# The mixer's 31-tap convolution, all four channel tiles on TensorE with dense weights in groups of 32 channels

## The chip, the cores and the metric

The kernel runs on one core of one Trainium2 chip. The metric is the device time of one execution, in microseconds; smaller is better.

## The reference

Two transformer blocks follow each other on one sequence of 512 tokens, model width 1024, all in float32. The change is inside the second block's mixer. There the normed input is projected to queries, keys and values of a differential attention (4 heads, two softmaxes per head whose difference weighs the values, a rotary embedding on 16 of 64 dimensions) and to `u`, 1024 columns for a convolution branch:

```python
    c = u[..., :CV_WIDTH] * jax.nn.sigmoid(u[..., CV_WIDTH:])      # CV_WIDTH = 512
    c = causal_dwconv(c, cv_dw_w) + cv_dw_b.astype(c.dtype)         # 31 taps, one filter per channel
    c = jax.nn.silu(layernorm(c, cv_ln_g, cv_ln_b))
    y = jnp.concatenate([a, c], axis=-1)                            # a: the attention's output
    return jnp.einsum("bsc,cd->bsd", y, w_out)
```

## The kernel before

Activations lie transposed, channels on the 128 partitions and the 512 tokens along the free axis, so the 512 convolution channels are four tiles. Every float32 matrix product is three TensorE matmuls: each operand is split into a high part (the value cast to fp32r) and a low part (the rest), and high x high, high x low and low x high are added in PSUM. A 128x512 step of a projection is three matmuls of 512 columns; a weight unit of 128x1024 feeds 24 of them.

Weights come as such units, in the order of `unit_order` (L192). A ring of four slots holds them: SP loads `raw` (L2809, 512 KB), ScalarE casts it to `wh` (`hi`, L1379), GpSimd subtracts to get `wl` (`low`, L2710), and each of them may start on unit j + 4 once TensorE has used unit j (`refill`). SP works off one list in unit order; what else it has to move is put in front of a certain `raw(j)`, and that `raw(j)` waits until `wl` of unit j - 4 is there. So a DMA in front of `raw(p + 9)` is issued after `wl` of unit p + 4.

No planner decides anything: each engine has its program written out by hand, and the order of the calls is the order of its queue. The calls of one name in the five programs (`dproj`, `qk_d`, `turn_d`, `pv_d`) are one step's share on each engine.

The stretch in question goes as follows.

- **u and dv** (TensorE L907 to L918). Four times two projections `u(j)`, `u(4+j)` go to PSUM banks (0,1), (2,3), (4,5), (0,1). VectorE multiplies each by the norm's factor (L2363), ScalarE takes the sigmoid, VectorE multiplies the two. After tile 1 VectorE also scales X (`scale_x`, eight operations). `dv` makes the values in banks 2 to 5; `v_low` on VectorE makes their low parts.
- **The convolution.** Tiles 0 and 1 are done by VectorE: `taps(m)` (L2349) does m multiply-adds of 512 elements, 62 in all, spread over the steps. Tiles 2 and 3 are done by TensorE with diagonal weights: 31 taps x 3 matmuls of 512 columns for each, on shifted views of a padded tile, in sixteen halves (`cw`, L936) called as `conv(x)` between other work, two of them ahead of step 0's `qk_d(2)`, eleven in steps 0 to 8, the last in step 10.
- **Query and key projections** `dproj(h, step)` (L920, L2387): steps 0 and 1 are the halves of dq, 3 and 4 those of dk, all in bank 0. After step 1 ScalarE copies the bank to `rx` and issues four small DMAs that exchange rows for the rotary embedding (L1677); VectorE multiplies by the cosines (to TM5), then in step 2 by the sines, adds, casts, subtracts. After step 4 ScalarE copies to `rth`, VectorE makes `rtl`, and TensorE's step 5, the rotation ("rot"), multiplies by a permutation; the same four VectorE operations follow.
- **The attention loop** of 16 steps n (head n // 4, row block n % 4; L1073, L1735, L2486). In step n TensorE does `qk_d(n + 2)`, half a projection while n < 10, and `turn_d(n)`, the transpose of the weights; in even steps also `pv_d(n // 2 - 1)`. ScalarE does the exponentials of n + 2, copies the transpose (`ath`) and scales for n + 1; VectorE the maxima of n + 2, the low part of the transpose (`atl`) and the difference of the two softmaxes of n + 1. `pv_d` needs `atl` of both of its steps. From step 10 on, keys and values of the memory fill TensorE's time.
- After step 9 the layer norm adds the four convolved tiles `AC`.

Of the kernel before, what the change touches and what calls it, by code (L numbers as in the profile page):

```python
# [7 lines left out]
F32 = mybir.dt.float32  # L8
# [7 lines left out]
P = 128  # L16
# [152 lines left out]
CW_HALVES = (2, 2, 1, 1, 1, 1, 1, 1, 1, 0, 1, 0, 0, 0, 0, 0)  # L169

KV_STEP = 10
CW_BEFORE = 4
TAP_STEPS = (3, 3, 3, 3, 3, 3, 2, 2, 0, 0, 0, 0, 0, 0, 0, 0)
assert CW_BEFORE + sum(CW_HALVES) == 16

# [16 lines left out]
def unit_order():  # L192
# [18 lines left out]
    done = CW_BEFORE  # L211
    for n in range(16):
        step = D_STEP.get(n, (0, 0))
        more = [("cw", 2 + x // 8, x // 2 % 4) for x in range(done, done + CW_HALVES[n]) if x % 2]
        done += CW_HALVES[n]
        u += [(("dq", "dk")[step[1] // 3], step[0])] if step[1] in (1, 4) else []
        u += more
        u += kv_units(n - KV_STEP) if n >= KV_STEP else []
# [19 lines left out]
TAPS = [tuple(range(8 * q, min(8 * q + 8, 31))) for q in range(4)]  # L238
# [7 lines left out]
def build(nc, args):  # L246
# [95 lines left out]
    CPF = at("cpf", [P, 2, T + 30], F32)  # L342
    ac0 = off[0]
    off[0] += 4096
    cp1 = off[0]
    CPAh = at("cpah", [P, 2, T + 30], F32R)
    cp2 = off[0]
    CPAl = at("cpal", [P, 2, T + 30], F32R)
    o_ac, o_yc = (ac0, ac0 + 2048, cp1, cp1 + 2176), (cp0, cp0 + 2176, cp2, cp2 + 2176)
    AC = [at(f"ac{j}", [P, T], F32, o_ac[j]) for j in range(4)]  # L350
# [25 lines left out]
    YCl = [at(f"ycl{j}", [P, T], F32R, o_ac[j]) for j in range(4)]  # L376

# [24 lines left out]
    def sig(name, step=1):  # L402
# [12 lines left out]

    s_wh, s_wl, s_unit = sig("s_wh"), sig("s_wl"), sig("s_unit")
# [24 lines left out]
    s_ux, s_us, s_cp, s_cph, s_cpl, s_pad, s_tap, s_ac = (  # L441
        sig(n) for n in ("s_ux", "s_us", "s_cp", "s_cph", "s_cpl", "s_pad", "s_tap", "s_ac"))
# [48 lines left out]
    def tensor_program(pe):  # L491
# [414 lines left out]

        for j in range(4):  # L907
# [27 lines left out]

        def cw(j, q, part):  # L936

            s = PLACE["cw", j, q] % RING
            if part == 0:
                if q == 0:  # L940
                    take(1)
                    pe.wait_ge(s_pad, 2)
                    pe.wait_ge(s_cpl, j)
                pe.wait_ge(s_wh, ("cw", j, q))
            for x in TAPS[q][4 * part:4 * part + 4]:
                w = slice(128 * (x % 8), 128 * (x % 8) + 128)
                pe.mm(PS[1][:, :], WH[s][:, w], CPAh[:, j - 2, x:x + T], x == 0, False)
                pe.mm(PS[1][:, :], WH[s][:, w], CPAl[:, j - 2, x:x + T], False, False)
                pe.wait_ge(s_wl, ("cw", j, q))
                last = pe.mm(PS[1][:, :], WL[s][:, w], CPAh[:, j - 2, x:x + T], False, x == 30)  # L950
            if part == 1:
                last.then_inc(*s_unit.up(("cw", j, q)))
                if q == 3:
                    bank[1] = (s_ac, (j,))
# [94 lines left out]
        def conv(x):  # L1049
            cw(2 + x // 8, x // 2 % 4, x % 2)  # L1050

        def filler(n):
            for x in range(cw_done(n), cw_done(n + 1)):
                conv(x)
            if n >= KV_STEP:
                kv(n - KV_STEP, 0)
# [3 lines left out]
        conv(0)  # L1060
        dproj(0, 2)
        conv(1)
        dproj(0, 3)
        dproj(0, 4)
        conv(2)
        dproj(0, 5)
        conv(3)
# [5 lines left out]
        for n in range(16):  # L1073
# [4 lines left out]
            if n % 2 == 0:  # L1078
                if n < KV_STEP:
                    filler(n)  # L1080
                if n == KV_STEP:
                    conv(15)
# [272 lines left out]
    def cw_done(n):  # L1355

        return CW_BEFORE + sum(CW_HALVES[:n])

# [19 lines left out]
    def scalar_program(act):  # L1378
# [47 lines left out]
        def vproj(br, nm, dh):  # L1426
            for u in range(4):
                if u == 3:
                    for t in v_rows(br):
# [11 lines left out]
                        elif br == "b":  # L1441
                            act.fn(heads(VB, t, 0), per_head(PS[2 + t]), ACT.Copy).then_inc(*s_vh.up(br, t))
                        else:
                            act.fn(dh[:, t, :], PS[2 + t][:, :], ACT.Copy).then_inc(*s_vh.up(br, t))
                if nm != "av" or u >= 2:
                    refill((nm, u))
# [187 lines left out]

        for j in range(4):
            if j:
                refill(("u", j))
                refill(("u", 4 + j))
            act.wait_ge(s_ux, j, 1)
            act.fn(u_tile(j, 1)[:, :], u_tile(j, 1)[:, :], ACT.Sigmoid).then_inc(*s_us.up(j))  # L1640
        vproj("d", "dv", V2h)

        def conv(x):
            conv_out(x)
            if x % 2:
# [284 lines left out]
    def vector_program(dve):  # L1930
# [411 lines left out]
        def scale_x(fs):  # L2342
            for f in fs:
                dve.wait_ge(s_root, "m2", "out")
                dve.stt(X[:, f, :], X[:, f, :], pcol("final_g", f), YF[:, 0, :], ALU.mult, ALU.mult).then_inc(*s_xn.up(f))

        taken = []

        def taps(m):  # L2349

            for n in range(len(taken), min(len(taken) + m, 62)):
                j, x = n // 31, n % 31
                taken.append(n)
                i, w = CPF[:, j, x:x + T], pcol("cv_dw_w_2", 4 * x + j)
                dve.wait_ge(s_pad, 0)
                dve.wait_ge(s_cp, j)
                if x == 0:
                    dve.ts(AC[j][:, :], i, w, ALU.mult, pcol("cv_dw_b_2", j), ALU.add).then_inc(*s_tap.up(j, x))
                    continue
                dve.wait_ge(s_tap, j, x - 1)  # L2360
                dve.stt(AC[j][:, :], i, w, AC[j][:, :], ALU.mult, ALU.add).then_inc(*s_tap.up(j, x))

        for j in range(4):  # L2363
# [3 lines left out]
            dve.tt(t1, PS[b0][:, :], RB[:, :], ALU.mult).then_inc(*s_ux.up(j, 0))  # L2367
            dve.wait_ge(s_unit, ("u", 4 + j))
# [3 lines left out]
            if j < 2:  # L2372
                dve.tt(CPF[:, j, 30:30 + T], t1, t2, ALU.mult).then_inc(*s_cp.up(j))
            else:
                dve.tt(t1, t1, t2, ALU.mult).then_inc(*s_cp.up(j))
                dve.wait_ge(s_cp, j)
                dve.cp(CPAh[:, j - 2, 30:30 + T], t1).then_inc(*s_cph.up(j))
                dve.wait_ge(s_cph, j)
                split_low(CPAl[:, j - 2, 30:30 + T], t1, CPAh[:, j - 2, 30:30 + T], (j,), s_cpl)
            if j == 1:  # L2380
                spread_out("m2", 6, YF[:, 0, :])
                scale_x(range(KC))
            taps((0, 6, 6, 14)[j])
# [66 lines left out]
        def ln_add(j):  # L2450
            if j == 1:
                dve.wait_ge(s_tap, 0, 30)
                dve.wait_ge(s_tap, 1, 30)
# [17 lines left out]

        dproj(0, 1)
        taps(3)
        dproj(0, 2)
        taps(3)
        dproj(0, 4)
        taps(3)
        dproj(0, 5)
        taps(3)
# [4 lines left out]
        taps(2)  # L2484
        join_d(0)
        for n in range(16):  # L2486
# [21 lines left out]
            taps(TAP_STEPS[n])  # L2508
# [12 lines left out]
        assert len(taken) == 62  # L2521
# [187 lines left out]
    def pool_program(pool):  # L2709
# [56 lines left out]
        pool.zero(CPF[:, :, 0:30]).then_inc(*s_pad.up(0))  # L2766
        pool.zero(f32(CPAh[:, :, 0:30])).then_inc(*s_pad.up(1))
        pool.zero(f32(CPAl[:, :, 0:30])).then_inc(*s_pad.up(2))
# [39 lines left out]
    def sync_program(sp):  # L2808
# [36 lines left out]

        b0 = PLACE["bq", 1] + 2 * RING
        for j in range(N_ADA + RING, len(UNITS)):
# [62 lines left out]
def pack_units(order, w):  # L2910
# [11 lines left out]
    for n, u in enumerate(order):  # L2922
# [25 lines left out]
        elif k == "cw":  # L2948
            b = np.zeros((128, U), np.float32)
            for i, x in enumerate(TAPS[u[2]]):  # L2950
                np.fill_diagonal(b[:, 128 * i:128 * i + 128], w["cv_dw_w_2"][0][x, 128 * u[1]:128 * u[1] + 128])
# [58 lines left out]
```

## Time and profile before

| | us |
|---|---|
| median of 3 runs | 1279.83 (1279.47 to 1279.92) |
| the profiled execution | 1277.17, span 1275.4 |
| TensorE matmul busy | 1239.7 (97%) |
| VectorE, ScalarE, GpSimd busy | 776.0, 590.5, 753.3 |
| granted TensorE clock, mean | 0.996 |

Times of the trace are in us from the span's start. Busy time of TensorE includes the pipelined end of each matmul (a 512-column one is shown with 0.39 us though the next starts 0.23 us after it), so the distance of starts is its rate. A wait of an engine is listed with the instruction that ended it. The work of the section above lies between 508 us (end of `u(4)`) and 678 us (`pv_d(4)`).

### The profile page before, as it was taken

How to read it: one execution, taken by the hardware profiler on the slowest of the kernel's cores; microseconds unless marked ns; L12 is line 12 of the kernel's file. 1: busy time of each engine (PE TensorE's matmuls, PEld its weight loads, DVE VectorE, ACT ScalarE, POOL GpSimd, SP SyncE). 2: the span in 40 equal slices, each digit the busy share in tenths (PEclk: the TensorE clock that was granted, in tenths of full speed). 3: DMA queues.
4: the chain of work that ended last, by engine and by line, in shares of the span. 5: the costliest groups of instructions: out<-in, count | busy, mean ns of one | idle time of the engine just before them, and what ended most of it. 6: DMA issues, size and time to landing. Idle time of an engine off the chain costs nothing.

```text
span 1275.4 us, 16982 instructions
## 1 busy us (share of the span) xinstructions
PE 1239.7 (97%) x6162; PEld 1032.8 (81%) x6162; DVE 776.0 (61%) x1271; ACT 590.5 (46%) x964; POOL 753.3 (59%) x864
## 2 busy tenths in 40 slices
PE   5999999999999999999999999999999999999997
PEld 4777878878888888887778988887888888888887
DVE  5868788436554466798877436764367516641654
ACT  3375667457774446233456654444334323331341
POOL 2634444434344676686446977436559958875782
PEclk9999999999999999999999999999999999999998
DMA  9422224232345633232224443212313332333322
GB/s 379 180 67 76 85 83 140 97 100 87 121 132 191 215 111 99 83 101 86 85 69 163 138 146 116 83 50 82 93 58 108 116 108 84 98 100 99 99 83 67
DMA packets 43108, 142.73 MB, mean 112 GB/s; under 512 B 4881, under 2 KB 7441, under 8 KB 41873
## 3 DMA queue, kind: packets, MB, share of 16 engines
q1 hardware_dynamic: 42768, 141.39, 34.1%
q8 instruction: 49, 0.80, 0.3%
q10 hardware_dynamic: 256, 0.26, 0.1%
q14 instruction: 35, 0.28, 0.1%
HBM read 130.88 MB, written 8.39 MB: 109 GB/s over the span
## 4 chain that ended last, share of the span: by engine, by line
PE 70%; DVE 20%; ACT 6%; issue 3%; POOL 1%; DMA 1%; DVEq 0%; SPq 0%; ACTq 0%; POOLq 0%
PE ps L126 69%; DVE tm L139 5%; ACT tm L133 3%; DVE tm L136 3%; DVE ma L139 1%; DVE ac L139 1%; ACT L133 1%; PE ps L130 1%; DVE spl L136 1%; DVE sph L147 1%; DVE tm L144 1%; DVE x L139 1%; DVE ewl L136 1%; DVE zh L147 1%; DMA x<-xin 1%
## 5 line engine op out<-in xcount | busy, mean ns | idle before, releaser
L136 POOL TENSOR_TENSOR wl<-raw,wh 128x256 fp32r<-128x256 f32 x804 | 695.8, 897 | 463.8 <-ACT wh L133 456.2
L133 ACT ACTIVATE wh<-raw 128x1024 fp32r<-128x1024 f32 x201 | 212.1, 1056 | 307.2 <-PE ps L126 301.3
L126 PE MATMUL ps<-hh,wh 128*128 128x512 f32 x872 | 344.2, 395 | 0.0
L126 PE MATMUL ps<-hh,wl 128*128 128x512 f32 x872 | 340.4, 390 | 0.0
L126 PE MATMUL ps<-hl,wh 128*128 128x512 f32 x872 | 340.4, 390 | 0.0
L126 PEld LDWEIGHTS ps<-hh,wl 128*128 128x128 f32 x872 | 164.1, 188 | 34.8
L126 PEld LDWEIGHTS ps<-hh,wh 128*128 128x128 f32 x872 | 164.2, 188 | 33.3 <-DVE tm L139 0.4
L126 PEld LDWEIGHTS ps<-hl,wh 128*128 128x128 f32 x872 | 164.3, 188 | 33.0
L139 DVE SCALAR_TENSOR_TENSOR tm<-cb,par_sb,tm 128x512 f32<-128x512 f32 x88 | 87.1, 990 | 50.5 <-ACT tm L133 47.1
L136 DVE TENSOR_TENSOR tm<-tm,tm 128x512 f32<-128x512 f32 (+4 forms) x113 | 93.3, 830 | 40.1 <-ACT tm L133 37.3
L133 ACT ACTIVATE tm<-tm 128x512 f32<-128x512 f32 (+3 forms) x109 | 54.1, 531 | 80.4 <-DVE tm L139 64.3
L136 DVE TENSOR_TENSOR x<-ps,x 128x512 f32<-128x512 f32 (+1 forms) x44 | 28.0, 638 | 86.0 <-PE ps L126 83.6
L126 PE MATMUL ps<-zh,wh 128*128 128x512 f32 (+1 forms) x200 | 73.0, 365 | 0.2 <-DVE x L136 0.2
L126 PE MATMUL ps<-zl,wh 128*128 128x512 f32 (+1 forms) x200 | 72.8, 364 | 0.1
L126 PE MATMUL ps<-zh,wl 128*128 128x512 f32 (+1 forms) x200 | 72.7, 364 | 0.0
L133 ACT ACT_TABLE_LOAD x50 | 64.2, 1283 | 14.2 <-DVE stat L150 7.4
L139 DVE SCALAR_TENSOR_TENSOR ac<-cpf,par_sb,ac 128x512 f32<-128x512 f32 x60 | 59.4, 990 | 1.6
L133 ACT ACTIVATE tm<-ps,stat 128x256 f32<-128x256 f32 (+3 forms) x80 | 40.4, 515 | 36.0 <-DVE stat L150 35.9
L136 DVE TENSOR_TENSOR cb<-ps,rb 128x512 f32<-128x512 f32 x44 | 30.1, 683 | 28.8 <-PE ps L126 28.7
L133 ACT ACTIVATE tm<-cb,par_sb 128x512 f32<-128x512 f32 x44 | 31.2, 710 | 29.8 <-DVE cb L136 29.8
L126 PEld LDWEIGHTS ps<-zl,wh 128*128 128x128 f32 x200 | 37.7, 189 | 6.5 <-POOL zl L136 0.6
L126 PEld LDWEIGHTS ps<-zh,wh 128*128 128x128 f32 x200 | 37.7, 189 | 6.5 <-DVE x L136 0.6
(308 smaller groups left out, 2254.0 us busy)
## 6 DMA issues: line engine op xcount, KB each, us to landing
raw<-units SPq DMA_DIRECT2D x201, 512.0 KB, 3.5
ada<-units SPq DMA_DIRECT2D x16, 512.0 KB, 14.7
kept<-ge SPq DMA_DIRECT2D x16, 256.0 KB, 3.0
tm<-kept SPq DMA_DIRECT2D x16, 256.0 KB, 3.7
tm<-gate_w SPq DMA_DIRECT2D x12, 256.0 KB, 4.2
x<-xin SPq DMA_DIRECT2D x2, 1024.0 KB, 6.3
x<-xin SPq DMA_DIRECT2D x1, 2048.0 KB, 11.2
out<-x SPq DMA_DIRECT2D x16, 128.0 KB, 1.8
```

What stands on the lines that cost most here:

```text
L126: return self.none if self.e is None else self.e.matmul(out, lhs, rhs, start=start, stop=stop, skip_group_check=skip)
L130: return self.none if self.e is None else self.e.transpose(out, in_, ident)
L133: return self.none if self.e is None else self.e.activation(out, in_, func, **kw)
L136: return self.none if self.e is None else self.e.tensor_tensor(out, a, b, op)
L139: return self.none if self.e is None else self.e.scalar_tensor_tensor(out, a, s, b, op0, op1)
L144: return self.e.tensor_scalar(out, a, s1, s2, op0) if op1 is None else self.e.tensor_scalar(out, a, s1, s2, op0, op1)
L147: return self.none if self.e is None else self.e.tensor_copy(out, in_)
```

## The change

All four tiles of the convolution go to TensorE. A tile's 128 channels are four groups g of 32. SP spreads the padded tile (high and low part, `USh` and `USl`) by eight DMAs so that partition block a (32 partitions) holds the channels shifted by 4a tokens (`MVh`, `MVl`: 32 channels x 4 groups). A dense 128x128 weight block then does 16 taps for four token phases m at once: rows 32a + c, columns 32m + c hold tap 4a + m + 16o, o = 0, 1. A product gives, on partition block m, the share of those taps; four gather DMAs take block m from `E`, shifted by m tokens, to `TT[m]`, and VectorE adds the four and the bias (`join`). Per group there are 2 offsets x 2 column halves x 3 = 12 matmuls of 258 columns. VectorE copies the banks to `E`.

The weight units of the convolution are four instead of eight and stand between the u and dv units; the convolution has left the d projections and the attention loop. The taps, and ScalarE's two bias copies, are gone. Some semaphore updates are left out below.

```diff
-    u += [("u", 4 * x + j) for j in range(4) for x in range(2)]
-    u += [("dv", i) for i in range(4)]
-    u += [("dq", 0), ("cw", 2, 0), ("dk", 0), ("cw", 2, 1), ("dq", 1)]
+    u += [("u", 0), ("u", 4), ("u", 1), ("u", 5), ("u", 2), ("cw", 0), ("u", 6), ("u", 3), ("cw", 1), ("u", 7)]
+    u += [("dv", 0), ("cw", 2), ("dv", 1), ("dv", 2), ("cw", 3), ("dv", 3)]
+    u += [("dq", 0), ("dk", 0), ("dq", 1)]
...
+        def conv(j, part):                          # TensorE
+            s, p = PLACE["cw", j] % RING, j % 2
+            if part == 0:
+                pe.wait_ge(l_mv[p], j, 3, 1)
+                pe.wait_ge(s_wh, ("cw", j))
+            for g in (2 * part, 2 * part + 1):
+                banks = conv_banks(j, g)
+                for b in banks:
+                    take(b)
+                for o in (0, 1):
+                    w = slice(256 * g + 128 * o, 256 * g + 128 * o + 128)
+                    cols = [slice(258 * y + 16 * o, 258 * y + 16 * o + 258) for y in range(2)]
+                    for y, b in enumerate(banks):
+                        pe.mm(PS[b][:, 0:258], WH[s][:, w], MVh[p][:, g, cols[y]], o == 0, False)
...
         for j in range(4):
+            if j >= 2:
+                conv(j - 2, 0)
             if j:
                 hproj("m", ("u", 4 + j), b1)
             bank[b1] = (s_ux, (j, 1))
-        vproj("d", "dv", "m")
+            if j >= 2:
+                conv(j - 2, 1)
+        def conv_beside(u):
+            if u:
+                conv(2 + u // 3, (u + 1) % 2 if u < 3 else 0)
+        vproj("d", "dv", "m", conv_beside)
+        conv(3, 1)
...
+    def conv_banks(j, g):
+        other = (2, 3) if j < 2 else (0, 1)
+        return ((6, 7), other)[g % 2] if g < 2 else (other, (6, 7))[g % 2]
...
+        def join(j):                                # VectorE
+            dve.wait_ge(l_tt[j % 2], j, 3)
+            dve.stt(AC[j][:, :], TT[0][:, :], pcol("cv_dw_b_2", j), TT[1][:, :], ALU.add, ALU.add)
+            dve.tt(TT[2][:, :], TT[2][:, :], TT[3][:, :], ALU.add)
+            dve.tt(AC[j][:, :], AC[j][:, :], TT[2][:, :], ALU.add)
+        def conv_out(j, part):
+            for g in (2 * part, 2 * part + 1):
+                for y, b in enumerate(conv_banks(j, g)):
+                    dve.cp(E[j % 2][:, g, 258 * y:258 * y + 258], PS[b][:, 0:258])
...
-            taps((0, 6, 6, 14)[j])
+            if j >= 2:
+                conv_out(j - 2, 1)
+        join(0)
+        conv_out(2, 0)
+        join(1)
+        conv_out(2, 1)
+        conv_out(3, 0)
+        join(2)
         v_low("d", V2h, V2l)
...
+        conv_out(3, 1)
         dproj(0, 1)
-        taps(3)
+        join(3)
         dproj(0, 2)
...
+        def spread_rows(j):                         # SP
+            sp.wait_ge(s_cpl, j)
+            if j == 1:
+                sp.wait_ge(s_xn, 7)
+            if j >= 2:
+                sp.wait_ge(s_unit, ("cw", j - 2))
+            for a in range(4):
+                for x, (mv, us) in enumerate(((MVh[p], USh[p]), (MVl[p], USl[p]))):
+                    sp.dma(f32(mv[GROUP * a:GROUP * a + GROUP, :, :]),
+                           f32(us[:, 4 * a:4 * a + CONV_IN]))
+        def gather_rows(j):
+            if j:
+                sp.wait_ge(s_ac, j - 1)
+            sp.wait_ge(s_e, j, 3, 1)
+            for m in range(4):
+                sp.dma(TT[m][:, :], E[p][GROUP * m:GROUP * m + GROUP, :, m:m + T])
...
+            for n, unit in enumerate((("u", 4), ("u", 5), ("u", 6), ("u", 7))):
+                if j == PLACE[unit] + 2 * RING + 1:
+                    if n >= 2:
+                        gather_rows(n - 2)
+                    spread_rows(n)
+            for n, unit in ((2, ("dv", 1)), (3, ("dv", 3))):
+                if j == PLACE[unit] + 2 * RING + 1:
+                    gather_rows(n)
```

## Rows read from the trace of the kernel before

**Rows 1.** The page: busy time, chain by engine, GpSimd's `wl` group (mean ns).

```profile
PE 1239.7 (97%) x6162; PEld 1032.8 (81%) x6162; DVE 776.0 (61%) x1271; ACT 590.5 (46%) x964; POOL 753.3 (59%) x864
PE 70%; DVE 20%; ACT 6%; issue 3%; POOL 1%; DMA 1%; DVEq 0%; SPq 0%; ACTq 0%; POOLq 0%
L136 POOL TENSOR_TENSOR wl<-raw,wh 128x256 fp32r<-128x256 f32 x804 | 695.8, 897 | 463.8 <-ACT wh L133 456.2
```

**Rows 2.** Windows: length, busy by engine (instructions), clock, DMA; last, taps alone.

```profile
497.00:612.70 115.70, 115.70 (x544) 94.41 (x543) 88.13 (x119) 36.82 (x57) 76.55 (x83) 1.00 0.30 92
612.70:678.00 65.30, 62.29 (x339) 49.02 (x337) 53.40 (x108) 32.16 (x72) 27.95 (x32) 1.00 0.31 99
616.10:678.10 62.00, 59.08 (x326) 46.90 (x326) 50.17 (x104) 30.68 (x70) 26.26 (x31) 1.00 0.31 98
...
616.10:678.10 62.00, 16.13 (x19) 0.00 (x0) 1.00 0.31 98
```

**Rows 3.** The chain that ended last, one of its tap pieces: start, us, what.

```profile
617.42 1.15 DVE ac L139
```

**Rows 4.** TensorE in order of time: start, us, engine, line, operation.

```profile
625.20 0.39 PE L126 MATMUL ps<-cpal,wh 128*128 128x512 f32 x1
625.43 0.39 PE L126 MATMUL ps<-cpah,wl 128*128 128x512 f32 x1
...
630.65 0.28 PE L126 MATMUL ps<-ath,v2h 128*128 128x256 f32 x1
630.77 0.28 PE L126 MATMUL ps<-atl,v2h 128*128 128x256 f32 x1
```

**Rows 5.** ScalarE and VectorE in order of time, u projections.

```profile
531.58 1.06 ACT L133 ACTIVATE wh<-raw 128x1024 fp32r<-128x1024 f32 x1 [4.38 <-PE ps L126]
...
523.14 0.68 DVE L147 COPY yf<-ps 128x512 f32<-128x512 f32 x1
523.85 8.26 DVE L139 SCALAR_TENSOR_TENSOR x<-x,par_sb,yf 128x512 f32<-128x512 f32 x8
```

**Rows 6.** DMA: six loads of 256 KB; the queue's rate in windows (last column); GpSimd.

```profile
tm<-kept SPq DMA_DIRECT2D x6, 256.0 KB, 4.9
...
406.00:408.00 2.00, 2.00 (x10) 1.67 (x9) 0.00 (x0) 0.00 (x0) 2.00 (x4) 1.00 0.63 187
...
744.00:746.00 2.00, 2.00 (x10) 1.44 (x9) 1.62 (x3) 1.04 (x2) 2.00 (x2) 1.00 1.00 356
...
20.00:22.00 2.00, 1.76 (x8) 1.79 (x9) 1.88 (x4) 0.00 (x0) 2.00 (x2) 1.00 1.03 410
...
582.43 4.18 POOL L136 TENSOR_TENSOR wl<-raw,wh 128x256 fp32r<-128x256 f32 x4 [1.67 <-ACT wh L133]
```

**Rows 7.** ScalarE after dproj(1,1): DMA issues, table load, last exp.

```profile
593.08 2.61 ACTq L159 DMA_DIRECT2D rs<-rx  x4
595.78 1.28 ACT L133 ACT_TABLE_LOAD   x1 [1.78 <-DVE stat L150]
...
597.43 0.36 ACT L133 ACTIVATE tm<-ps,stat 128x128 f32<-128x128 f32 x1
```

**Rows 8.** VectorE after a key projection; ScalarE and VectorE after a query's.

```profile
643.55 1.28 DVE L150 TENSOR_REDUCE stat<-ps 128x1 f32<-128x512 f32 x2
...
647.33 0.42 DVE L136 TENSOR_TENSOR atl<-ps,ath 128x256 fp32r<-128x256 f32 x1
...
656.34 0.58 ACT L133 ACTIVATE rx<-ps 128x512 f32<-128x512 f32 x1
...
656.94 2.64 ACTq L159 DMA_DIRECT2D rs<-rx  x4
...
661.24 0.69 DVE L136 TENSOR_TENSOR atl<-ps,ath 128x512 fp32r<-128x512 f32 x1 [0.65 <-ACT ath L133]
```

**Rows 9.** TensorE near the kernel's start, two neighbouring matmuls.

```profile
31.81 0.63 PE L126 MATMUL ps<-wh,hl 128*128 128x512 f32 x1
32.23 0.63 PE L126 MATMUL ps<-wh,hh 128*128 128x512 f32 x1
```

More of the change, by code:

```diff
@@ L1 @@
+import itertools
 from contextlib import ExitStack
@@ L236 @@
 OFF = [0, 512, 896, 1152]
-TAPS = [tuple(range(8 * q, min(8 * q + 8, 31))) for q in range(4)]
+GROUP = 32
+CONV_IN = 532
+CONV_OUT = 516
 C1 = 6.28125
@@ L341, in build @@
     cp0 = off[0]
[L342 to L350, printed above, removed]
+    PADDED = T + 32
+    USh = [at(f"ush{i}", [P, PADDED], F32R) for i in range(2)]
+    USl = [at(f"usl{i}", [P, PADDED], F32R) for i in range(2)]
+    o_yc = [cp0 + 4 * PADDED * j for j in range(4)]
+    o_ac = [off[0] + 2048 * j for j in range(4)]
+    AC = [at(f"ac{j}", [P, T], F32) for j in range(4)]
+    off[0] += 256
     LM = at("lm", [P, 384], F32, cp0 + 6912)
@@ L376, in build @@
     YCl = [at(f"ycl{j}", [P, T], F32R, o_ac[j]) for j in range(4)]
+    g0, mv = dq0 + 640, 16 * CONV_IN
+    MVh, MVl = ([at(f"mv{n}{i}", [P, 4, CONV_IN], F32R, (v20, yf0 + 3072)[i] + x * mv) for i in range(2)]
+                for x, n in enumerate("hl"))
+    E = [at(f"e{i}", [P, 4, CONV_OUT], F32, g0 + 16 * CONV_OUT * i) for i in range(2)]
+    RB2 = at("rb2", [P, T], F32, yf0 + 1024)
+    TT = [at(f"tt{i}", [P, T], F32, sq0 + 2048 * i) for i in range(4)]
     off[0] = b2
@@ L904, in tensor_program @@
         bank[7] = (s_root, ("m", "out"))
+        def conv(j, part):
[12 more added lines that the diff above has]
+                        pe.mm(PS[b][:, 0:258], WH[s][:, w], MVh[p][:, g, cols[y]], o == 0, False)
+                    for y, b in enumerate(banks):
+                        pe.mm(PS[b][:, 0:258], WH[s][:, w], MVl[p][:, g, cols[y]], False, False)
+                    pe.wait_ge(s_wl, ("cw", j))
+                    for y, b in enumerate(banks):
+                        last = pe.mm(PS[b][:, 0:258], WL[s][:, w], MVh[p][:, g, cols[y]], False, o == 1)
+                last.then_inc(*(s_unit.up(("cw", j)) if g == 3 else s_conv.up(j, g)))
+                for y, b in enumerate(banks):
+                    bank[b] = (s_e, (j, g, y))
         for j in range(4):
@@ L934, in dproj @@
             bank[b] = (s_rx, (nm, h, 2))
[L936 to L954, printed above, removed]
         def qk_d(n):
@@ L1424, in scalar_program, with vproj @@
                 refill(("av", 1))
-        def vproj(br, nm, dh):
+        def vproj(br, nm, dh, between=None):
             for u in range(4):
+                if between:
+                    between(u)
                 if u == 3:
@@ L1444, in vproj @@
                             act.fn(dh[:, t, :], PS[2 + t][:, :], ACT.Copy).then_inc(*s_vh.up(br, t))
+                if br == "d" and u == 3:
+                    conv_out(3, 1)
                 if nm != "av" or u >= 2:
@@ L1632, in scalar_program @@
         refill(("u", 4))
+        def conv_out(j, part):
+            if part:
+                refill(("cw", j))
         for j in range(4):
@@ L2483, in vector_program @@
         dproj(1, 2)
-        taps(2)
         join_d(0)
@@ L2765, in pool_program @@
         pool.wait_ge(s_unit, ("wo", 7))
-        pool.zero(CPF[:, :, 0:30]).then_inc(*s_pad.up(0))
-        pool.zero(f32(CPAh[:, :, 0:30])).then_inc(*s_pad.up(1))
-        pool.zero(f32(CPAl[:, :, 0:30])).then_inc(*s_pad.up(2))
+        for p in range(2):
+            for t in (USh[p], USl[p]):
+                pool.zero(f32(t[:, 0:30]))
+                last = pool.zero(f32(t[:, 30 + T:PADDED]))
+        last.then_inc(*s_pad.up(2))
         pool.zero(RS[:, :]).then_inc(*s_pad.up(3))
@@ L2949, in pack_units @@
             b = np.zeros((128, U), np.float32)
-            for i, x in enumerate(TAPS[u[2]]):
-                np.fill_diagonal(b[:, 128 * i:128 * i + 128], w["cv_dw_w_2"][0][x, 128 * u[1]:128 * u[1] + 128])
+            taps = w["cv_dw_w_2"][0][:, 128 * u[1]:128 * u[1] + 128]
+            c = np.arange(GROUP)
+            for g, o, a, m in itertools.product(range(4), range(2), range(4), range(4)):
+                x = 4 * a + m + 16 * o
+                if x < 31:
+                    b[GROUP * a + c, 256 * g + 128 * o + GROUP * m + c] = taps[x, g::4]
         elif k == "wo2":
```

124 lines of the change are left out of this document (42 added, 82 removed).

## The prediction

> **What bounds the kernel now.** I read the page's head first: TensorE is busy 97% of the span, VectorE 61%, and the chain that ended last is 70% TensorE, 20% VectorE [rows 1]. Then the windows of the stretch that the change touches [rows 2]. From 497 to 612.7 us TensorE has no gap; in 612.7 to 678 it is busy 62.3 of 65.3 us, so 3.0 idle, and the chain there goes through VectorE and ScalarE, where single taps stand between a softmax and the next [rows 3]; after 678 TensorE is full again. So two things bound this stretch: TensorE's matmuls, and a serial path through ScalarE and VectorE that the convolution's matmuls cover at present.
>
> **What the change takes from TensorE and gives it.** Out go 186 matmuls of 512 columns (31 taps, two tiles, three each), one every 0.23 us [rows 4], 0.234 with what begins each half: 43.5 us. In come 4 tiles x 4 groups x 2 offsets x 2 halves x 3 = 192 matmuls of 258 columns. The nearest rows are the 256-column ones, one every 0.12 us [rows 4]; I take 0.1185, 22.8 us in all, 2.85 us for each of the eight half tiles (as much as twelve old ones). By the same rows it could be 22.4 to 24.5. Net -20.7 us, if TensorE never waits.
>
> **What it takes from the others.** VectorE loses 62 taps (990 ns each, some 61 us), of which 16.1 us lie in 616.1 to 678.1 [rows 2]; it gets 32 bank copies (about 0.4 us each: 0.68 for a 512-wide read of PSUM, 0.42 for a 256-wide one [rows 5, 8]), three adds per tile (about 2.1 us) and two more splits. Four weight units go, 3.6 us of GpSimd and 1.06 of ScalarE each, both hidden now. None of this counts by its sum: VectorE has room. It counts by where it stands in the queues.
>
> **New waits in the u and dv projections.** The old end of a unit is where ScalarE's conversion starts: u6 531.6, u2 one unit of 5.4 earlier [rows 5]. With conv(0,0) put in, u6 ends at 534.5 and conv(0,1) wants banks 2 and 3. VectorE has the added split of tile 1 (1.65 us) and then 8.26 us of scale_x first [rows 5], until 533.8, then one multiply and four copies, until 536.1: wait 1.6. After u7, dv0 wants bank 2, which conv(1,1) fills: ScalarE converts (1.06), sigmoid, VectorE multiplies, splits, copies, 4.5 us after u7 against 2.9 of convolution: wait 1.7. dproj(0,0) wants bank 0; VectorE's copy is behind join(2), which waits for gather(2). SP has that behind a raw load that waits for wl of dq0: convolution ends 574.0, ScalarE 1.1, GpSimd 2 x 3.6 (897 ns x 4 [rows 1]), so issued at 582.9, landed 5 us later (six 256 KB loads: 4.9 [rows 6]), then 2.1 of adds, 2.7 of v_low and a copy: 593.1 against 590.7, wait 2.4 (3.5 at the 4.2 us that a unit takes GpSimd around there [rows 6]).
>
> **New waits in the first d projections.** The four convolution halves between them are gone, 5.4 us of projection remain per unit, all in bank 0. dproj(0,3) waits for ScalarE's copy and VectorE's multiply: 1.5. Then rot(0), at 605.6: VectorE has join(3) in front of dproj(0,2); gather(3) is on SP behind the raw load that waits for wl of dk1 (from cw3's end at 590.9: one conversion 1.1, two units of GpSimd 7.2: 599.2), lands about 604.4; join 2.1, the four operations of dproj(0,2) 2.9, split and multiply of dproj(0,4) 1.3: 610.7, wait 5.1. Queued behind join(3) is thus all of head 0's query and key. dproj(1,0) waits 0.8 for the multiply after rot. qk_d(2) waits for the exps: at present dproj(1,1) ends at 592.4, the fourth DMA issue on ScalarE's queue at 595.7, then come a table load of 1.28 and two exps with their sums until 597.8 [rows 7], 5.4 us after the projection, against 1.4 of qk_d: wait 4.0, covered now by two convolution halves. rot(1): 1.2.
>
> **New waits in the attention loop.** Two patterns repeat. (a) After a key projection: rot waits for the multiply into TM5; from that multiply's end VectorE still has two reductions, four operations of dproj(h,5) and the low part of the transposed weights before pv_d may start: 643.6 to 647.8, 4.2 us [rows 8], with 0.9 of rot and transpose beside it, so 3.4 to 3.5 idle. (b) After dproj(h,1): ScalarE copies, spends 2.64 us issuing four DMAs, only then does the exps of qk_d(n+2), then ath, then VectorE atl: from 656.3 to 661.9 in the one case where no tap is in the way, 5.6 us, and 0.1 from the last matmul to the copy [rows 8]. TensorE has qk and transpose, 1.1 to 1.5 us: idle 4.6 and 4.2. Laid end to end pv_d(0) to pv_d(4) takes 13.2 + 14.8 + 13.2 + 14.8 = 56.0 us, against 616.1 to 678.1 = 62.0 now: eight halves, 22.8 us, leave and 6.0 is gained. Idle: pv_d(0) 3.4, then 4.6 + 3.5 + 4.2 + 3.5 = 15.8. After pv_d(4) nothing changes; the memory halves land 7.2 us after dk3, 6.6 before pv_d(4), and are used 1.8 after it.
>
> **The sum.** Waits: 1.6 + 1.7 + 2.4 + 1.5 + 5.1 + 0.8 + 4.0 + 1.2 + 3.4 + 15.8 = 37.5; the 3.0 idle of now are in them. -20.7 + 37.5 - 3.0 = +13.8 us. The profiled execution took 1277.17 us for a span of 1275.4, so 1291; it is 2.7 below the median of 1279.83, and on the median it is **1293.6 us**. Ends of the unknown costs: the loop 52 to 59, copies and GpSimd +-2, matmuls -0.4 to +1.7, gathers +-2: 1288 to 1299 for this case.
>
> **The transfers.** Each tile is spread by eight DMAs (2.18 MB) to 32 partitions each and gathered by four (1.05 MB). At 300 GB/s, under the 410 of the loads at the start and the 356 of kv's move inside SBUF [rows 6], and 2 us for the landing, spread(0), ready at 515.9, lands by 525.5 for 526.1; spread(1), at 533.8 behind scale_x, by 543.1 for 544.4; spread(2) behind gather(0) by 562 for 562.8. I take no wait; the margin is 0.6 to 1.3 us. No row shows a DMA with 32 partitions on one side.
>
> **Rivals.** First: the spreads land late. At the 187 GB/s that the queue moved while six 256 KB loads were being issued [rows 6] a spread takes 11.7 us plus 2: spread(0) is 3.5 late (in the place of the 1.6 at conv(0,1)), spread(1) 3, spread(2) and spread(3), behind a gather, about 2 each after what the first lateness has shifted: +8, **1302**. For it: the narrow margins; against: 356 GB/s in a move inside SBUF [rows 6]. The Trainium skill, "SBUF — State Buffer", section "Door 1: The DMA port swizzle", has it that 32 partitions reach 8 of 16 ports and about 218 GB/s; that is this rival, and no run here shows it yet. By its figure a spread takes 10.0 us and 2, and the sum would be +6 for the +8.
>
> Second: TensorE's clock falls in the new gaps. Behind the idle time at the start of the kernel seven matmuls came 0.42 us apart (1.2 GHz) and from there on 0.23 (2.4 GHz) [rows 4, 9], 1.4 us lost. Four of my gaps have 4.0 us or more; 1.4 lost at each is 5.6, some of it hidden, about +5: **1299**. Against: the gaps have work on both sides.
>
> Third, on the other side: the loop goes at TensorE's pace. VectorE's work without taps is 50.2 - 16.1 = 34.1 us in the 62.0, ScalarE's 30.7, TensorE's 62 - 22.8 - 3 = 36 [rows 2]; if the engines overlap as these sums allow, as where pv_d's two inputs come before TensorE has reached it, the loop takes 40 us instead of 56, and the total is about 2 us faster; if gather(3) is also early and the exps of qk_d(2) are hidden, 9 more: **1269 to 1278**. It decides at one point: whether atl of step 4h+3 ends less than 2 us after the projection before it. Against it stands the fixed order of ScalarE's queue [rows 8].
>
> Fourth: the waits come to just what the matmuls give back, 1278 to 1282, if the loop takes 48 us and join(3) is 4 us earlier.
>
> **Chances.** Forecast 0.50 (1288 to 1299), late spreads 0.17, clock 0.12, faster 0.13, evened out 0.08. Slower by over 0.2% (2.6 us, about what can be told from no change here): 0.50 + 0.17 + 0.12 + a quarter of the last = 0.81; within: 0.05; faster: 0.14. The range, with 2 in 10 outside, is 1279 to 1304: it takes in half of the evened-out case and both slower rivals.
>
> **What would show it.** Right: matmuls of the new kind 0.12 us apart; TensorE without the old 100% in 600 to 690; idle before pv_d laid to atl, 3 to 5 us at four or five places; 54 to 58 us from pv_d(0) to pv_d(4); VectorE's wait for tt from its DMA before 606; u5 to dv0 longer by convolution and 3 us. Wrong: waits of TensorE for mv tiles (first rival), a granted clock under 1.0 between 590 and 700 (second), or pv_d starting with no idle before it (third).

## The result and the profile after

The changed kernel takes 1333.01 us (median of 4 runs, 1331.43 to 1337.44), the one before 1279.65 on the same chip (1279.11 to 1279.92): a ratio of 1.0423, 95% interval 1.0396 to 1.0451. So it is slower by 53.4 us, where 13.8 were forecast. The profiled execution took 1334.48 us with a span of 1332.4, 57.0 more than the span of before.

The page's head and its DMA issues (last column: median us from issue to landing), to be laid beside [rows 1, 6]:

```profile
PE 1243.1 (93%) x6168; PEld 1038.3 (78%) x6168; DVE 737.8 (55%) x1257; ACT 586.6 (44%) x958; POOL 723.9 (54%) x853
...
PE 69%; DVE 17%; ACT 5%; DMA 3%; issue 3%; POOL 2%; SPq 2%; ACTq 0%; DVEq 0%; POOLq 0%
...
mvh<-ush SPq DMA_DIRECT2D x16, 266.0 KB, 10.0
mvl<-usl SPq DMA_DIRECT2D x16, 266.0 KB, 11.2
...
tt<-e SPq DMA_DIRECT2D x16, 256.0 KB, 5.1
```

TensorE's busy time has not fallen, though by the forecast's count 20.7 us of work were taken out: at the lower clock a matmul of 512 columns starts 0.43 us after the one before it, not 0.23. DMA and SP's queue have come into the chain, where they were 1% and 0%. Two pieces of it (start, us, what) are spreads on their way:

```profile
537.81 16.87 DMA mvl<-usl
...
588.75 11.00 DMA mvl<-usl
```

Windows of the changed kernel, columns as in [rows 2]; the last three numbers are the granted clock, the DMA engines' share and GB/s:

```profile
497.00:630.00 133.00, 107.13 (x552) 91.60 (x552) 50.19 (x90) 27.80 (x33) 57.15 (x82) 0.93 0.83 173
630.00:740.00 110.00, 79.67 (x381) 62.76 (x382) 56.76 (x134) 43.93 (x101) 20.26 (x27) 0.76 0.17 55
518.00:520.00 2.00, 2.00 (x10) 1.65 (x10) 0.00 (x0) 0.00 (x0) 0.00 (x0) 1.00 1.05 121
526.00:528.00 2.00, 0.00 (x0) 0.00 (x0) 2.00 (x4) 0.79 (x1) 1.05 (x1) 1.00 1.12 130
528.00:530.00 2.00, 0.00 (x0) 0.00 (x0) 2.00 (x3) 0.00 (x0) 2.00 (x3) 0.78 1.05 126
530.00:534.00 4.00, 0.00 (x0) 0.00 (x0) 3.33 (x4) 0.00 (x0) 1.52 (x2) 0.50 1.07 126
```

Two things are to be seen, and both are rivals of the prediction. While the first spreads are under way the DMA engines are full (a share of 1.05 to 1.12) and move only 121 to 130 GB/s. And the clock, 1.00 in both stretches before, is 0.76 over 110 us: within one wait of 8.9 us in which TensorE does nothing it goes from 1.00 (2.4 GHz) to 0.50 (1.2 GHz).

TensorE's waits from 497 to 760 us (us in total, times, the longest):

```profile
PE ps L127 <- DVE atl L137: 19.1, 5, 4.5
PE ps L127 <- DMA mvl<-usl: 17.7, 4, 8.9
PE ps L127 <- DVE tm L140: 12.4, 4, 9.2
PE ps L127 <- ACT tm L134: 4.1, 1, 4.1
PE ps L127 <- DVE e L148: 2.6, 2, 1.6
```

And the places themselves, in order of time (start, us, what, the wait before it in brackets):

```profile
515.07 0.69 SPq L160 DMA_DIRECT2D mvh<-ush  x1
...
519.71 0.62 SPq L160 DMA_DIRECT2D mvl<-usl  x1
...
534.59 0.80 PE L127 MATMUL ps<-mvh,wh 128*128 128x258 f32 x2 [8.90 <-DMA mvl<-usl]
...
545.38 0.40 PE L127 MATMUL ps<-mvl,wh 128*128 128x258 f32 x2
545.62 0.40 PE L127 MATMUL ps<-mvh,wl 128*128 128x258 f32 x2
...
619.01 4.35 SPq L160 DMA_DIRECT2D tt<-e  x4
...
619.34 4.61 ACTq L160 DMA_DIRECT2D rs<-rx  x4
...
634.99 0.77 PE L127 MATMUL ps<-rth,conr 128*128 128x512 f32 x1 [9.17 <-DVE tm L140]
...
637.56 0.63 PE L127 MATMUL ps<-hl,wh 128*128 128x512 f32 x1
637.99 0.63 PE L127 MATMUL ps<-hh,wl 128*128 128x512 f32 x1
...
665.99 0.55 PE L127 MATMUL ps<-ath,v2h 128*128 128x256 f32 x1 [3.52 <-DVE atl L137]
...
682.14 0.55 PE L127 MATMUL ps<-ath,v2h 128*128 128x256 f32 x1 [4.54 <-DVE atl L137]
...
732.02 0.55 PE L127 MATMUL ps<-ath,v2h 128*128 128x256 f32 x1 [3.72 <-DVE atl L137]
```

The pairs of 258 columns at 545 are 0.24 us apart, 0.12 a matmul, as forecast. Those of 512 at 637 are 0.43 apart, as at the kernel's start [rows 9]. From pv_d(0) to pv_d(4) it takes 66.0 us; the forecast was 56.0, and before it was 62.0.

### The profile page after: what moved, and what is told of

It reads as the page before. It is cut to its first block, busy times and chain, and to the rows that moved or that the text cites. A ratio compares the mean times of both kernels' runs of the same rounds, so it can differ in the third digit from the quotient of the medians.

```text
span 1332.4 us, 17010 instructions
## 1 busy us (share of the span) xinstructions
PE 1243.1 (93%) x6168; PEld 1038.3 (78%) x6168; DVE 737.8 (55%) x1257; ACT 586.6 (44%) x958; POOL 723.9 (54%) x853
## 4 chain that ended last, share of the span: by engine, by line
PE 69%; DVE 17%; ACT 5%; DMA 3%; issue 3%; POOL 2%; SPq 2%; ACTq 0%; DVEq 0%; POOLq 0%
PE ps L127 67%; DVE tm L140 4%; ACT tm L134 2%; DVE tm L137 2%; DMA mvl<-usl 2%; SPq L160 2%; POOL wl L137 1%; DVE ma L140 1%; PE ps L131 1%; ACT L134 1%; DVE x L140 1%; DVE spl L137 1%; DVE sph L148 1%; DVE tm L145 1%; DVE ewl L137 1%
## 5 line engine op out<-in xcount | busy, mean ns | idle before, releaser
L137 POOL TENSOR_TENSOR wl<-raw,wh 128x256 fp32r<-128x256 f32 x788 | 666.1, 877 | 550.2 <-ACT wh L134 534.9
L134 ACT ACTIVATE wh<-raw 128x1024 fp32r<-128x1024 f32 x197 | 207.8, 1056 | 353.1 <-PE ps L127 347.2
L127 PE MATMUL ps<-hh,wh 128*128 128x512 f32 x872 | 347.8, 399 | 3.8 <-DVE tm L140 2.2
L137 DVE TENSOR_TENSOR cb<-ps,rb 128x512 f32<-128x512 f32 x44 | 30.1, 684 | 28.7 <-PE ps L127 28.6
L127 PEld LDWEIGHTS ps<-zh,wl 128*128 128x128 f32 x200 | 37.7, 189 | 5.9
## 6 DMA issues: line engine op xcount, KB each, us to landing
mvl<-usl SPq DMA_DIRECT2D x16, 266.0 KB, 11.2
```

The lines of the kernel that those rows point to most:

```text
L127: return self.none if self.e is None else self.e.matmul(out, lhs, rhs, start=start, stop=stop, skip_group_check=skip)
L134: return self.none if self.e is None else self.e.activation(out, in_, func, **kw)
L137: return self.none if self.e is None else self.e.tensor_tensor(out, a, b, op)
```

## The experiments

The theory to be tested (A): the ten waits of the forecast are right, and what it lacks is the two rivals, late spreads (because their target is 32 partitions wide) and TensorE's clock behind gaps. The rival (B) differs from run to run and stands in each expectation. Most variants were run two to four times, and waits and windows are read from one profiled execution of each. "The kernel before" took 1279.06 to 1279.69 us beside these runs.

**The clock, in the loop.** 115 matmuls of 512 columns on constants go where TensorE waits, into a bank that nothing reads.

```diff
+        def fill(b, k):
+            take(b)
+            for _ in range(k):
+                pe.mm(PS[b][:, :], con_r("o128"), conr[:, 0:T], True, True)
...
         dproj(0, 4)
+        fill(1, 30)
         dproj(0, 5)
...
         qk_d(1)
+        fill(1, 15)
...
+                if n and n <= KV_STEP:
+                    fill(1, {2: 12, 4: 18, 6: 12, 8: 16, 10: 12}[n])
                 if n:
                     pv_d(n // 2 - 1)
```

> The changed kernel with extra 128x512 matmuls of a constant tile into bank 1, whose result nobody reads, put where TensorE stands idle: 30 before the first rotation, 15 before qk_d(2), and 12, 18, 12, 16, 12 before pv_d(0) to pv_d(4). Theory A (the idle gaps halve TensorE's clock, and that is what the forecast of the loop missed): granted clock 1.0 from 630 us on, pv_d(0) to pv_d(4) 56 to 58 us instead of 66.0, total 12 to 18 us faster than the changed kernel, 1316 to 1321, though 115 matmuls are added. Theory B (the loop is longer because its chain through ScalarE and VectorE is longer than I took it): the extra matmuls change nothing, or cost a few us, 1331 to 1336.

It took 1318.43 us (1314.23 to 1322.62), ratio 1.0298 (1.0216 to 1.0379). The window of the loop, and the first and last pv_d:

```profile
630.00:740.00 110.00, 104.09 (x643) 84.59 (x641) 67.25 (x156) 55.60 (x124) 34.73 (x46) 1.00 0.23 74
```

```profile
658.12 0.36 PE L127 MATMUL ps<-ath,v2h 128*128 128x256 f32 x1 [0.76 <-DVE atl L137]
...
714.56 0.36 PE L127 MATMUL ps<-ath,v2h 128*128 128x256 f32 x1 [1.00 <-DVE atl L137]
```

More work makes it faster by 14.6 us at the median, with the two runs 8.4 us apart (1314.23 and 1322.62) and both below the fastest of the changed kernel, 1331.43. The clock is 1.00 in this window, and the loop takes 56.4 us, the forecast's 56.0: the chain through ScalarE and VectorE, which the filler does not touch, was priced rightly, and the other 9.6 us are matmuls at 1.2 GHz.

**join(3) later.** It goes behind dproj(0,5) on VectorE, so that head 0's query and key are not queued behind gather(3).

```diff
         dproj(0, 1)
-        join(3)
         dproj(0, 2)
         dproj(0, 4)
         dproj(0, 5)
+        join(3)
```

> The changed kernel with VectorE's join(3) behind dproj(0,5) instead of ahead of dproj(0,2). Theory A (join(3), which waits for the last gather, holds up query and key of head 0): TensorE's wait before the first rotation falls from 9.2 us to about 3, and the clock stays up for what follows, total 6 to 10 us faster, 1323 to 1327. Theory B (the rotation waits for the small row DMAs on ScalarE's queue, which stand behind the gathers on the DMA engines): the wait stays at 9, total within 1 us of the changed kernel.

1329.85 us (1327.67 to 1332.03), ratio 1.0387 (1.0339 to 1.0434): its interval overlaps the changed kernel's, so the total shows no clear gain. The wait at the rotation falls from 9.17 to 5.11 and does not go. In order of time:

```profile
620.37 4.15 ACTq L160 DMA_DIRECT2D rs<-rx  x4
...
627.57 0.69 DVE L140 SCALAR_TENSOR_TENSOR tm<-rs,stb 128x512 f32<-128x512 f32 x1 [6.51 <-DMA rs<-rx]
...
631.96 0.76 PE L127 MATMUL ps<-rth,conr 128*128 128x512 f32 x1 [5.11 <-DVE tm L140]
```

ScalarE's four small DMAs took 4.15 us to issue (4.61 with join(3) in its place) against 2.61 before [rows 7], and landed 7.2 us after the first issue (627.57) against 4.2 in the kernel before. gather(3) was on its way at the same time, from 621.86; the three later exchanges of the changed kernel, with no gather beside them, take 2.61 to 2.64 us to issue. The late spreads are not needed for this meeting: the forecast's own times put dproj(0,1)'s end at about 598.5 and gather(3) at 599.2. Both theories hold in part: 4 us of that wait were join(3)'s, and what is left stands behind the exchange of rows. That the gather is what slows the exchange was not tested apart.

**The width of the target.** The same bytes in as many DMAs go to all 128 partitions. Left out: the right input of the convolution.

```diff
-                    sp.dma(f32(mv[GROUP * a:GROUP * a + GROUP, :, :]),
+                    sp.dma(f32(mv[:, a, :]),
                            f32(us[:, 4 * a:4 * a + CONV_IN])).then_inc(...)
```

> The changed kernel, but each spread DMA writes its 128 rows of 2128 bytes to 128 partitions instead of to four places on 32 partitions (the convolution's input is then not the right one). Same bytes, rows, starts and count. Theory A (the narrow target is what makes a spread take 19.5 us): a spread of 2.18 MB takes 7 to 9 us, TensorE's 17.7 us of waits for it go, total 18 to 25 us faster, 1308 to 1315. Theory B (rows of 2128 bytes between SBUF tiles, or their starts off a multiple of 64 bytes, are slow whatever the target): still 18 to 20 us, total unchanged.

The profiled execution took 1309.18 us against 1334.48; it is the only one to compare, since the second run of this kernel, 3141.73 us, is left aside. Its page and two windows:

```profile
mvh<-ush SPq DMA_DIRECT2D x16, 266.0 KB, 3.1
mvl<-usl SPq DMA_DIRECT2D x16, 266.0 KB, 3.2
```

```profile
518.00:520.00 2.00, 2.00 (x11) 1.65 (x10) 0.00 (x0) 0.00 (x0) 0.96 (x2) 1.00 1.05 401
...
630.00:740.00 110.00, 89.56 (x538) 75.25 (x537) 59.87 (x140) 53.76 (x120) 35.11 (x45) 0.86 0.21 69
```

Landing takes 3 us instead of 10 to 11, the DMA engines move 401 GB/s instead of 121, no wait for mv is left, and 25 us are gone, as theory A has it. The gaps before pv_d stay at 19.1 us in all and the loop at 65.6 us, with the clock at 0.81 from pv_d(0) to pv_d(4) (0.78 in the changed kernel; the window above ends 33 us behind it): what is lost there is not the transfers'.

**What about the narrow target.** Three variants of it. First, all DMAs read from the same column, so that shifted starts play no part (`us[:, 0:CONV_IN]`; the right input is left out).

> The changed kernel, but every spread DMA reads from the tile's first element instead of from element 4a (again not the right input), still onto 32 partitions. Theory A (narrow target): the spread still takes 18 to 20 us, total within 2 us. Theory B (the start of the source row, 16, 32 or 48 bytes in, costs): it takes about 10 us or less, total 10 us faster or more.

1335.71 us (1333.09 to 1338.34), its interval over the changed kernel's, and the first wait still 8.9: not the shift. Second, the same DMAs in an order in which neighbours write partition blocks 0 and 2, and 1 and 3.

```diff
-            for a in range(4):
-                for x, (mv, us) in enumerate(((MVh[p], USh[p]), (MVl[p], USl[p]))):
+            for a, x in ((0, 0), (2, 0), (0, 1), (2, 1), (1, 0), (3, 0), (1, 1), (3, 1)):
```

> The changed kernel with the spread DMAs in another order: partitions 0, 64, 0, 64, 32, 96, 32, 96 instead of 0, 0, 32, 32, 64, 64, 96, 96 (the result is the same). Theory A (each DMA engine works off its queue in order, and within one DMA of 32 target partitions the engines hold each other up): a spread still takes 19 us, total 1330 to 1335. Theory B (the limit is the half of the target that is written, and neighbours in the queue could overlap): a spread takes 10 to 14 us, TensorE's wait for spread(0) falls from 8.9 to 1 to 4, total 8 to 15 us faster.

1327.11 us (1326.53 to 1327.69), ratio 1.0369 (1.0345 to 1.0392). Waits, and the page's landing times:

```profile
PE ps L127 <- DMA mvl<-usl: 13.1, 4, 8.9
```

```profile
mvh<-ush SPq DMA_DIRECT2D x16, 266.0 KB, 6.1
mvl<-usl SPq DMA_DIRECT2D x16, 266.0 KB, 8.6
```

This is 5.9 us faster, between the two theories' ranges: the first spread is as late as ever, and the later three gain 4.6 us of waits. Theory B's 10 to 14 us for a spread did not come; why the later ones gain is open. Third, 64 partitions (the rows go to two slots of partitions 0 to 63 or 64 to 127; the right input is left out).

> The changed kernel, but each spread DMA writes its 128 rows to two places on 64 partitions instead of four on 32 (not the convolution's right input). Theory A (64 neighbouring partitions reach no more of the write paths than 32): a spread still takes 19 us, total 1330 to 1335. Theory B (the rate goes with the number of target partitions): about 10 us a spread, as the wide one took 7.7, and the total within 6 us of the wide one's 1309.

1332.96 us (1332.31 to 1333.61), the first wait 8.82, landing 9.7 and 10.5 us: 64 partitions bring no more than 32 (10.0 and 11.2). The Trainium skill, "SBUF — State Buffer", "Door 1: The DMA port swizzle", says this of 0 to 63 and 0 to 31, and the trace agrees; the page's 218 GB/s for either is not reached in these runs, where a spread onto 32 partitions moves 112. What else halves the rate when both ends lie in SBUF is open.

**The cover alone.** In the kernel before, 138 of the 186 convolution matmuls are left out (each half keeps its waits and one tap's three matmuls), 32.2 us of TensorE.

```diff
-            for x in TAPS[q][4 * part:4 * part + 4]:
+            for x in TAPS[q][4 * part:4 * part + 4][-1:]:
```

> The kernel before, of whose 186 convolution matmuls only the 48 of the last tap of each half are left (all units, conversions, waits, taps on VectorE and DMAs stay; the output is not the reference's): 138 matmuls, 32.2 us of TensorE, gone. Theory A (the convolution's matmuls cover a serial path through ScalarE and VectorE, and what is left idle slows the clock): pv_d(0) to pv_d(4) stays at 58 to 66 us, TensorE idles 20 us or more, the granted clock falls below 0.9 in 600 to 680, total 1268 to 1290. Theory B (that stretch is bound by TensorE's work): total 1247 to 1255.

1280.85 us (median of 10 runs, nine of them from 1278.09 to 1282.12, one 6018.75), ratio 1.0006 (0.9995 to 1.0016). Three windows and two of the waits:

```profile
560.00:600.00 40.00, 30.23 (x133) 23.21 (x131) 35.47 (x44) 13.46 (x22) 27.90 (x29) 0.90 0.32 99
600.00:640.00 40.00, 34.51 (x153) 26.46 (x150) 31.76 (x66) 18.16 (x42) 16.26 (x20) 0.80 0.24 78
640.00:690.00 50.00, 41.12 (x246) 33.43 (x245) 37.28 (x79) 29.68 (x60) 22.35 (x27) 0.90 0.31 107
```

```profile
PE ps L126 <- DVE atl L136: 11.8, 4, 3.2
PE ps L126 <- DVE tm L139: 7.9, 5, 4.9
```

32 us less for TensorE, and nothing gained, with no spread and no gather in it. The convolution's matmuls stood over a chain that takes its time without them, and they kept the clock up. From 560 to 690 us TensorE is busy 105.9 us, against 126.9 before: 21 us of the 32.2 have become idle time, and about 11 went into matmuls at the lower clock (0.87 over this stretch). What the chain alone would take, with the clock held up, was not run. Nor is it the changed kernel's chain: VectorE's taps for tiles 0 and 1 are still in it, 22% of the chain in this stretch, and the change takes them out. So taking matmuls away gains nothing by itself here; with the taps gone too and the clock at 1.00 the loop took 56.4 us against 62.0, which is the gain of about 6 us that the forecast gave it.

**Together, and more cover.** The wide spread, join(3) late and the filler, with 6 filler matmuls ahead of the rotation (the right input is left out):

> The changed kernel with the three causes taken away together: spreads to 128 partitions (not the convolution's right input), join(3) behind dproj(0,5), and extra matmuls into bank 1 in the gaps (6 before the first rotation, 15 before qk_d(2), 12, 18, 12, 16, 12 before the pv_d). Theory A (slow spreads, slow clock and the queue of join(3) are all that the forecast missed or priced, so what is left is its table of waits without the 5.1 at the rotation): 1286 to 1293. Theory B (something else in the new order costs too): 1297 or more.

1298.94 us (1295.59 to 1299.33), ratio 1.0141 (1.0119 to 1.0164). That is 5.9 us over theory A's range and inside theory B's: something else costs too. From 600 to 640 us the clock was still 0.91. The next run has 18 filler matmuls ahead of the rotation and 12 in bank 2 ahead of dproj(0,0) (`fill(1, 18)`, `fill(2, 12)`).

> The wide spread, join(3) behind dproj(0,5), and the loop's filler (that gave 1298.9 with 6 filler matmuls ahead of the rotation), now with 18 ahead of the rotation and 12 in bank 2 ahead of dproj(0,0). Left out: the wide spread does not bring the right input. Theory A, what stood above the forecast there (about 5 us) was the clock at 1.2 GHz in 600 to 640: dproj(1,0) and (1,1) take 5.5 us instead of 7.9, the rotation 0.5 instead of 2.0, dproj(0,0) 5.6 instead of 7.1, and the time is 1293 to 1296, the forecast's 1293.6 at the low end. Theory B, it is waits of their own, whatever the clock: 1298 to 1301.

1294.11 us (1291.84 to 1296.14), ratio 1.0118 (1.0101 to 1.0135). The window that had 0.91, TensorE at four places, and VectorE ahead of the rotation:

```profile
600.00:640.00 40.00, 34.34 (x171) 26.17 (x172) 22.97 (x48) 13.69 (x31) 12.21 (x16) 1.00 0.29 87
```

```profile
525.78 0.48 PE L127 MATMUL ps<-mvh,wh 128*128 128x258 f32 x2
...
607.90 0.69 DVE L140 SCALAR_TENSOR_TENSOR tm<-rs,stb 128x512 f32<-128x512 f32 x1 [7.10 <-DMA rs<-rx]
...
612.31 0.47 PE L127 MATMUL ps<-rth,conr 128*128 128x512 f32 x1 [1.59 <-DVE tm L140]
...
638.39 0.36 PE L127 MATMUL ps<-ath,v2h 128*128 128x256 f32 x1 [0.78 <-DVE atl L137]
...
694.83 0.36 PE L127 MATMUL ps<-ath,v2h 128*128 128x256 f32 x1 [0.99 <-DVE atl L137]
```

The time is inside theory A's range, so most of what stood above the last run's was the clock, and with the transfers and the clock taken away the kernel lands on the forecast of 1293.6, within 3 us at each place too (table below). That shows the two rivals to be the bulk of the miss, but part of the match is luck. In this run join(3) no longer stands ahead of the rotation, and the forecast had put a wait of 5.1 us down to it; without that term the forecast is 1288.5. Yet the rotation comes 18.5 us after dproj(0,0) starts (17.6 forecast, with join(3) in front), since VectorE waits until 607.90 for the exchange of rows, whose first issue was at 600.10. The size of that term was right, and its cause was not.

**The clock, in the convolution.** The filler of the first run, and 34, 3, 16 and 2 more in the waits for the spreads, transfers as they are:

> The changed kernel with the filler matmuls of the loop and of the rotation (115, as in the first experiment), and 55 more in the four waits for the spread tiles: 34, 3, 16 and 2 matmuls of 512 columns on constants, ahead of conv(0,0), conv(1,0), conv(2,0) and conv(3,0). The waits themselves stay (spread(0) still lands at about 534.5). Theory A, the clock's fall costs in every gap: conv(0,0) takes 2.9 us instead of 5.1, conv(2,0) 2.9 instead of 4.5, and what hangs on TensorE after them comes earlier, so 3 to 6 us less than with the loop's filler alone (1318.4): 1312 to 1316. Theory B, in this part what DMAs and other engines deliver sets the pace, and a faster convolution only waits longer at the next step: 1317 to 1320.

1320.08 us (1317.45 to 1322.08), ratio 1.0322 (1.0306 to 1.0337), at the upper end of theory B's range: nothing gained on the 1318.4 of the first experiment, as far as its two runs can tell.

```profile
535.37 0.51 PE L127 MATMUL ps<-mvh,wh 128*128 128x258 f32 x2 [1.13 <-DMA mvl<-usl]
...
557.81 0.80 PE L127 MATMUL ps<-mvh,wh 128*128 128x258 f32 x2 [4.78 <-DMA mvl<-usl]
```

conv(0,0) starts at full clock and takes 2.97 us instead of 5.09, and then conv(1,0) waits 4.78 us for spread(1) instead of 1.04. Among the spreads the transfers set the pace, and the clock costs little there. spread(1) landed 3 us later than in the changed kernel too; why was not looked into.

**The best that is whole.** DMAs in the other order, join(3) late and filler everywhere; nothing is left out.

> Nothing of the computation left out: the spread's DMAs in the other order, join(3) behind dproj(0,5), filler matmuls ahead of pv_d, qk_d(2) and the rotation (14) and in the waits for the spread tiles (34, 2, 6, 2). If the parts add up (4.2% slower for the change; about 15 us back by the loop's filler, 6 by the order, 3 by join(3), some by the filler ahead of the convolution): 1306 to 1312. If they overlap (the same microseconds under two names): 1313 to 1318. Both leave it slower than the kernel before by more than 2%, since the transfer of spread(0), some 9 us of wait, stays.

1314.32 us (1311.20 to 1316.08), ratio 1.0275 (1.0259 to 1.0291). The parts overlap: 18.7 us back, where by the expectation they would add up to 24 or more. It is still 35 us behind the kernel before. Moving the dense convolution into the loop, as cover, was not tried: its tiles have no room in SBUF there.

## Why the prediction was wrong

Slower was right. The size was wrong: 53.4 us instead of 13.8. Lateness against the forecast, in us (pv_d(4) is forecast at 678.1 + 13.8, pv_d(0) 56.0 before it; the last column is the run with all the cover, in which join(3) is moved too; the last row compares spans):

| | forecast | changed kernel | transfers and clock taken away |
|---|---|---|---|
| conv(0,0) starts | 526.1 | 534.59 (+8.5) | 525.78 (-0.3) |
| dproj(0,0) starts | 593.1 | 612.92 (+19.8) | 593.83 (+0.7) |
| rotation starts | 610.7 | 634.99 (+24.3) | 612.31 (+1.6) |
| pv_d(0) starts | 635.9 | 665.99 (+30.1) | 638.39 (+2.5) |
| pv_d(4) starts | 691.9 | 732.02 (+40.1) | 694.83 (+2.9) |
| span, above before | +13.8 | +57.0 (+43.2) | +17.1 (+3.3) |

- **The matmuls: right.** 0.12 us each, 2.89 us a half tile where the clock was full (forecast 2.85).
- **VectorE's copies, the new waits: mostly right.** Forecast against measured: dv0 1.7, 1.03; dproj(0,0) 2.4, 1.56; dproj(0,3) 1.5, 1.41; dproj(1,0) 0.8, 0.78; qk_d(2) 4.0, 4.14; rot(1) 1.2, 0.99; pv_d(0) 3.4, 3.52; then 4.6, 3.5, 4.2, 3.5 against 4.54, 3.72, 3.64, 3.72. conv(0,1)'s 1.6 did not appear, since the tile before it was late anyway (0.7 with the wide spread), and dproj(0,0)'s is 3.8 there, near the 3.5 that the forecast had in brackets. Only the rotation's 5.1 was 9.17: gather(3) landed 8.3 us after its first issue, where 5.2 were taken, and ScalarE's exchange, which the step left out, 7.8 us after its own, both at about 627.2, with join(3)'s adds behind them. The run with all the cover has a wait of the same size without join(3), behind the exchange alone.
- **"I take no wait" for the transfers: the step that failed first.** The rate was 2.18 MB in the 19.5 us from 515.07 to 534.59, 112 GB/s, where 300 were taken from a full-width move. The rival had the mechanism, and its price (+8) came from 187 GB/s, a row whose DMA engines were busy only 0.63 of the time and which therefore shows no limit of theirs. Its full price, by one execution with the wide spread, is 25 us, of which 17.7 are waits for mv: dproj(0,0) starts 18.8 us earlier there, and pv_d(0) 24.4. The prediction's own sentence that no row shows a narrow DMA should have made the rate's lower end much lower, and so the upper end of the range higher: a margin of 0.6 to 1.3 us could not carry it.
- **The clock: the step that failed second.** The rival priced four gaps at 1.4 us each. In the loop alone, the gaps of 3.5 to 4.6 us cost 9.6 us, since a part of what follows each runs at 1.2 GHz, and then comes the next gap: behind pv_d(0), the 24 matmuls of 512 columns of the projection take 7.6 us from the first start to the last (668.42 to 676.00), and 5.7 with the filler (659.50 to 665.20). From dproj(0,0) to pv_d(0) the changed kernel takes 53.1 us, the forecast 42.8 and the run with filler 47.3, so the clock gives 5.8 more there; all of the filler gave back 14.6. The argument "the gaps have work on both sides" was no argument. The Trainium skill, "TensorE: Matmul & The Clock Gate", "HAM oscillation — how this bites in real kernels", tells of a kernel whose waits, there for DMAs, come again and again, so that it starts cold behind each; the trace agrees in the main, with 0.76 over 110 us. Not behind every gap, though: after 3.64 us of waiting at 715.61 matmuls still start 0.12 us apart, and the clock falls only about 1.3 us after that.
- **The rivals were weighed one by one.** +8 and +5 as alternatives to each other, though the late spreads make gaps of their own, and the clock works in all of them; taken away together, with join(3) moved as well, they gave back 38.9 us, from 1333.0 to 1294.1.
- **The faster rival** fell with the loop's 56.4 us, where it had 40: ScalarE's and VectorE's order binds, and the run without cover points the same way.

## What to carry to other kernels

Before crediting work taken off the busiest engine, ask what its matmuls were covering: leave them out of the kernel before and time that (here 32 us less were worth 0 us, a third of it by the clock), and keep in mind what else the change takes out of the covered chain. Where the answer opens gaps of 3.5 us and more one after the other, reckon the matmuls behind each at the lower clock, or fill the gaps. And take the rate of a transfer only from a row with the same number of partitions at its narrow end; where there is none, measure it first. And take no limit from a row in which the DMA engines were not full.

## What was not expected of the hardware

- Moves within SBUF of 128 rows of 2128 bytes: 2.18 MB onto 32 partitions at a time in 19.5 us (112 GB/s), onto 64 about as slow (landing 9.7 and 10.5 us), onto 128 partitions in 7.4 us (516.05 to 523.4, 296 GB/s; 401 in the fullest 2 us).
- The issue of one spread DMA on SP's queue took about 0.61 us, narrow or wide, with single ones of 1.1 to 4.0; four small ones on ScalarE's queue took 4.15 to 4.61 us instead of 2.61 where gather(3) was being issued at the same time (3.64 us in the first run with filler, where the two overlapped in part, and 3.22 with the wide spread, where they followed it).
- 115 matmuls that compute nothing made this kernel 14.6 us faster.
